# Token-first gated branches and a token-first retention tail in a three-block transformer kernel

## Chip, cores and metric

The kernel runs on one core of a Trainium2 chip. The metric is the device time of one execution in microseconds (us); a smaller time is better. TensorE (PE) multiplies matrices, VectorE (DVE) and ScalarE (ACT) do element-wise work, SyncE (SP) issues the DMAs.

## What is computed

A batch of 256 tokens of width 1024 goes through one block with three gated branches (convolution, stick-breaking attention, cross attention to a memory) and then through two hybrid layers (softmax attention with forget gates, and retention). In the reference, the parts that the change touches are these:

```python
# first block
gates = jax.nn.sigmoid(gate_pre).reshape(b, s, N_BRANCH, d)
merged = gates[:, :, 0] * y_conv + gates[:, :, 1] * y_sb + gates[:, :, 2] * y_x
x = x + merged @ w_out[l]              # y_* are [256,1024] @ [1024,1024]
# each of two hybrid layers: 4 retention heads of 128
q_r = rotary(rq); k_r = rotary(rk) * (RET_HEAD_DIM ** -0.5)
ret = retention_chunkwise(q_r, k_r, rv, gamma)
ret = (ret - mean) * rsqrt(var + GN_EPS) * ret_gn_g      # per token and head
ret_out = jax.nn.silu(rg) * ret
mixed = concatenate([fox_out, ret_out], -1)
x = layernorm(ALPHA * x + mixed @ w_out)
x = layernorm(ALPHA * x + square(relu(x @ w_ff1)) @ w_ff2)
```

## The kernel before

Every weight matrix is cut into "halves" of 1 MB (128 partitions x 2048 values). SP loads a half into one of two slots of raw, ACT rounds it to w_hi (split, L331), DVE subtracts to get w_lo (L725), both in a ring of four. Activations are kept as such pairs too (H, R, Q), and each product is three: hi x hi, lo x hi, hi x lo. Half l is split while half l - 4 is finished; SP loads half l once lo_ready has reached l - 1, that is, once the low part of half l - 2, in the same slot, is done. The order on each engine is written out by hand and every queue runs in order.

A half is multiplied in one of two forms. rows_first (products at L1282) has the weights stationary and streams 256 tokens, so the output has features in partitions: 8 x 2 x 3 = 48 matmuls with 256 columns. tokens_part and tokens_half (L1321, L1322, L1327) have 128 tokens stationary and stream 512 weight columns, so the output has tokens in partitions: 4 x 2 x 3 = 24 matmuls with 512 columns. A token-first output needs two halves (both halves of the contraction) and two PSUM banks, one for each block m of 128 tokens; results go to a ring of three banks of gps.

First block: h runs over 64 halves. Halves 36 to 59 are the gated stretch: four pairs (gate, y) for each of the branches sb, x and conv. ACT turns the gate's bank into gate with a sigmoid (L557) and copies y's to staged (L347), DVE multiplies and adds into merged (L1073 to L1077), and for the last branch ACT and DVE make Q_hi and Q_lo of it (L565, L1083). Halves 60 to 63 are w_out, token-first, then mlp_norm. The heads of the cross attention (h = 35 to 40: scores, softmax on DVE and ACT at L1010 to L1021 and L511, transposes at L1479, values at L1490) and the last norms of its queries (head_rsqrt, L351 and L353) run between the first of these halves.

A hybrid layer: l runs over 16 halves, then w_out takes four (LWO = 16 to 19), then the MLP starts at LFFN = 20. Among the halves are: rotations of queries and keys (rotate(r), L1624, DVE at L1183 to L1186, two of them after l = 11), the retention scores and masks (L1719, L1192), retention_values (L1630, L1632; b = 0 after l = 14, b = 1 after l = 15), the gate projection rg (LRG = 14 and 15, rows-first). The retention's output ro has features in partitions, so mean and variance per head are sums over partitions: matmuls with a matrix of ones (L1640, L1645), in between w_out's first two halves; ACT squares, DVE centres (L1216), and the reciprocal root is taken on whole 128x512 tiles (L742 to L746, L351, L353). ACT and DVE then write Q_hi and Q_lo (L707, L1243), for which w_out's last two halves wait. SP loads the norm's rows (load_rows) after rn_o and gn_lo. DVE does split(LWO+3) after the two centrings; split(LFFN) and split(LFFN+1) come after the last Q_lo and ahead of layer_norm (L817 to L873). layer_norm's result is transposed by TensorE (L1345).

## Time and profile before

| | |
|---|---|
| median of 3 runs | 1312.22 us (1306.88 to 1312.27) |
| profiled execution | 1308.6 us, span 1306.8 us |
| granted TensorE clock, mean | 0.990 |
| TensorE busy | 1245.1 us (95%) |
| VectorE busy | 775.6 us (59%) |
| ScalarE busy | 616.4 us (47%) |
| loads of weight halves | 196 of 1 MB, mean 166 GB/s over the span |

A line of the timeline gives the start in the span, the duration, the engine, the line of the kernel, the operation and its tiles; in brackets stands the engine's idle time before it and what ended it. The chain is the work that ended last, followed back link by link. Back-to-back instructions overlap, so durations of neighbours can add up to more than the distance of their starts; the chain's pieces do not overlap.

### The profile page before, as it was taken

The numbers are of one execution on the slowest core, as the hardware profiler recorded it, in microseconds if no ns is written. First come the engines' busy times: TensorE is split into PE (matmuls) and PEld (weight loads), VectorE is DVE, ScalarE is ACT, GpSimd is POOL, SyncE is SP. The second block draws the span as 40 slices with busy tenths as digits, with TensorE's granted clock in tenths as the row PEclk, the third lists the DMA queues.
The fourth block names the chain that finished last, engine by engine and source line by source line (L and its number), as shares of the span: only waits on it lengthen the run. The fifth ranks groups of instructions, "written<-read, shape, count | busy, mean of one in ns | idle before, by whom it ended". The sixth has DMA issues, their size and how long they took to land.

```text
span 1306.8 us, 19708 instructions
## 1 busy us (share of the span) xinstructions
PE 1245.1 (95%) x8208; PEld 1124.8 (86%) x8208; DVE 775.6 (59%) x823; ACT 616.4 (47%) x676; POOL 0.2 (0%) x4
## 2 busy tenths in 40 slices
PE   5989999999999999999999989999998998899997
PEld 5979998989999899998787868989978886789896
DVE  5566875764555565555356586555566566765545
ACT  4555554664534454444254535544435434454441
POOL 0000000000000000000000000000000000000000
PEclk9989999999999999999999999999999999999999
DMA  6644344433655356554353334655525334365550
GB/s 214 219 158 162 127 164 144 179 125 134 214 203 181 129 212 207 193 183 171 114 202 108 148 139 166 222 181 199 169 94 194 129 129 177 130 209 193 193 193 32
DMA packets 33250, 216.88 MB, mean 166 GB/s; under 512 B 4384, under 2 KB 6432, under 8 KB 7456
## 3 DMA queue, kind: packets, MB, share of 16 engines
q1 hardware_dynamic: 33184, 215.92, 47.5%
q8 instruction: 51, 0.84, 0.3%
q14 instruction: 15, 0.12, 0.0%
HBM read 214.85 MB, written 1.05 MB: 165 GB/s over the span
## 4 chain that ended last, share of the span: by engine, by line
PE 75%; DVE 11%; DMA 6%; ACT 5%; issue 2%; SPq 0%; ACTq 0%; DVEq 0%
PE gps L1282 39%; PE aps L1321 7%; PE aps L1322 7%; PE aps L1327 7%; DMA raw<-w 6%; DVE w_lo L725 4%; PE gps L1321 3%; ACT w_hi L331 3%; PE gps L1322 3%; PE gps L1327 3%; PE aps L1432 1%; DVE B L873 1%; DVE rs L863 1%; DVE B L867 1%; DVE B L817 1%
## 5 line engine op out<-in xcount | busy, mean ns | idle before, releaser
L725 DVE TENSOR_TENSOR w_lo<-raw,w_hi 128x2048 fp32r<-128x2048 f32 x200 | 449.0, 2248 | 288.1 <-ACT w_hi L331 287.8
L331 ACT ACTIVATE w_hi<-raw 128x2048 fp32r<-128x2048 f32 x200 | 374.1, 1875 | 210.9 <-DMA raw<-w 122.1
L1282 PE MATMUL gps<-H_hi,w_hi 128*128 128x256 f32 x896 | 240.9, 290 | 12.5 <-ACT H_hi L366 5.7
L1282 PE MATMUL gps<-H_hi,w_lo 128*128 128x256 f32 x896 | 236.6, 285 | 0.0
L1282 PE MATMUL gps<-R_hi,w_hi 128*128 128x256 f32 x800 | 209.2, 283 | 0.0
L1282 PE MATMUL gps<-R_hi,w_lo 128*128 128x256 f32 x800 | 209.0, 283 | 0.0
L1282 PEld LDWEIGHTS gps<-H_hi,w_hi 128*128 128x128 f32 x896 | 174.1, 194 | 16.4 <-issue 12.9
L1282 PE MATMUL gps<-H_lo,w_hi 128*128 128x256 f32 x896 | 181.4, 285 | 0.0
L1282 PEld LDWEIGHTS gps<-H_hi,w_lo 128*128 128x128 f32 x896 | 174.1, 194 | 0.7 <-issue 0.5
L1321 PE MATMUL aps<-w_hi,Q_hi 128*128 128x512 f32 x416 | 162.2, 390 | 0.8 <-DVE Q_lo L923 0.8
L1322 PE MATMUL aps<-w_lo,Q_hi 128*128 128x512 f32 x416 | 162.1, 390 | 0.0
L1282 PE MATMUL gps<-R_lo,w_hi 128*128 128x256 f32 x800 | 160.5, 283 | 0.0
L1282 PEld LDWEIGHTS gps<-R_hi,w_lo 128*128 128x128 f32 x800 | 153.5, 192 | 0.8
L1282 PEld LDWEIGHTS gps<-R_hi,w_hi 128*128 128x128 f32 x800 | 153.4, 192 | 0.8
L1282 PEld LDWEIGHTS gps<-H_lo,w_hi 128*128 128x128 f32 x896 | 141.1, 194 | 0.0
L1282 PEld LDWEIGHTS gps<-R_lo,w_hi 128*128 128x128 f32 x800 | 124.5, 192 | 0.0
L1327 PE MATMUL aps<-w_hi,Q_lo 128*128 128x512 f32 x416 | 111.2, 389 | 0.0
L1321 PEld LDWEIGHTS aps<-w_hi,Q_hi 128*128 128x128 f32 x416 | 78.2, 188 | 16.5 <-DVE Q_lo L923 1.0
L1327 PEld LDWEIGHTS aps<-w_hi,Q_lo 128*128 128x128 f32 x416 | 78.1, 188 | 16.2
L1322 PEld LDWEIGHTS aps<-w_lo,Q_hi 128*128 128x128 f32 x416 | 78.2, 188 | 15.7
L406 ACT ACTIVATE staged<-gps 128x512 f32<-128x512 f32 x42 | 25.0, 596 | 103.6 <-PE gps L1282 103.6
L347 ACT ACTIVATE B<-gps 128x512 f32<-128x512 f32 x56 | 32.3, 588 | 72.2 <-PE gps L1282 63.3
(223 smaller groups left out, 1377.2 us busy)
## 6 DMA issues: line engine op xcount, KB each, us to landing
raw<-w SPq DMA_DIRECT2D x196, 1024.0 KB, 4.9
B<-rows SPq DMA_DIRECT2D x4, 1024.0 KB, 4.5
B<-x_t SPq DMA_DIRECT2D x2, 512.0 KB, 4.6
B<-mem_t SPq DMA_DIRECT2D x1, 1024.0 KB, 9.1
B<-x SPq DMA_DIRECT2D x1, 1024.0 KB, 7.7
B<-con SPq DMA_DIRECT2D x1, 1024.0 KB, 9.6
out<-B SPq DMA_DIRECT2D x4, 256.0 KB, 2.0
B<-rows SPq DMA_DIRECT2D x1, 512.0 KB, 6.2
```

What stands on the lines that cost most here:

```text
L331: act.activation(w_hi[:, ring(l), 0:n], raw[:, raw_slot(l), 0:n], ACT.Copy)\
L347: act.activation(dst, src, ACT.Copy, scale=scale).then_inc(s["evac"], 1)
L406: act.activation(staged[:, a, :], up_bank(par_, a), ACT.Relu)\
L725: dve.tensor_tensor(w_lo[:, ring(l), 0:n], raw[:, raw_slot(l), 0:n], w_hi[:, ring(l), 0:n].bitcast(F32), ALU.subtract)\
L817: ins = dve.scalar_tensor_tensor(t, t, scale, out, ALU.mult, ALU.add)
L863: st.mark(dve.bn_stats(stats[:, m, 6 * j:6 * j + 6], chunk(X, m, j)))
L867: st.mark(dve.scalar_tensor_tensor(t, t, stats[:, m, 12:13], g_row[:, 512 * j:512 * (j + 1)], ALU.subtract, ALU.mult))
L873: dve.scalar_tensor_tensor(t, t, stats[:, m, 17:18], b_row[:, 512 * j:512 * (j + 1)], ALU.mult, ALU.add).then_inc(s["t_z"], 1)
L1282: return pe.matmul(gps[:, bank_, nt * T:(nt + 1) * T], w[:, r, c:c + P], op[:, k, :], start=start, stop=stop, skip_group_check=True)
L1321: pe.matmul(out, x, w_hi[:, r, c], start=(start and k == ks[0]), stop=False)
L1322: pe.matmul(out, x, w_lo[:, r, c], start=False, stop=False)
L1327: ins = pe.matmul(out, op_lo[:, 4 * g + k, rows], w_hi[:, r, c], start=False, stop=(stop and k == ks[-1]))
```

## The change

The weights of gates and branch outputs are laid out for token-first products, in pairs of halves: for each branch and each 512 columns two halves of the gate, then two of y. All 24 halves become tokens_half. ACT evacuates both token blocks after the second half of a pair, DVE gates them into merged, now with tokens in partitions, and TensorE transposes merged (turn_merged: 8 transposes after half 56, 8 among w_out's first half) for Q_hi and Q_lo.

In the hybrid layers rg is token-first as well and stays in PSUM. retention_values gives tokens in partitions, both blocks after l = 15. Mean and variance come from bn_stats and bn_aggr per head, the root is taken on 4 values per token, ACT normalises with scale and bias per token, and DVE multiplies with the gate, which it has multiplied with the gain from gn_row (a new broadcast load of 256 KB per layer, which SP issues once fx_l has reached 4). TensorE transposes the result for Q_hi and Q_lo (turn_retention). The matmuls for mean and variance go, and the squares and the full-size Newton steps with them. DVE does split(LWO+3) after gn_gated. w_out's last two halves go block by block. rotate(2) uses its own bank and does not wait for rt_x any more. In the diff, removed lines are left out in the longer pieces; they are those of the kernel printed above.

```diff
@@ -293,8 +294,11 @@
                     sp.wait_ge(s["gn_lo"], 2 * ly)
                 sp.dma_start(lpar[:, :], par2[ly]).then_inc(s["lpar_loaded"], 16)
 
-                for i in range(2, 10):
+                for i in range(2, 9):
                     load_pair(i)
+                sp.wait_ge(s["fx_l"], 4 * ly + 4)
+                sp.dma_start(gn_row, rows3[ly:ly + 1, :].to_broadcast([P, 4 * P])).then_inc(s["gn_row_loaded"], 16)
+                load_pair(9)
                 sp.wait_ge(s["rn_o"], 2 * ly + 2)
                 load_rows(0)
                 load_pair(10)
+                    if (h - 36) % 4 == 1:
+                        for m in range(2):
+                            act.wait_ge(s["gemm_done"], h + 1)
+                            act.wait_ge(s["staged_free"], staged_n + m - 1)
+                            act.activation(gate[:, m, :], bank(h - 1 + m), ACT.Sigmoid).then_inc(s["evac"], 1)
+                    elif (h - 36) % 4 == 3:
+                        for m in range(2):
+                            act.wait_ge(s["staged_free"], staged_n - 1)
+                            evac(staged[:, m, :], bank(h - 1 + m), h + 1)
+                            staged_n += 1
                 elif h == WO1:
                     act.preload_act_table_set("natural_log_exp_and_others")
+                if h in (GATED["conv"] + 4, WO1):
+                    for m in range(2):
+                        j = int(h == WO1)
+                        act.wait_ge(s["mg_tr"], 2 * j + m + 1)
...
                     if l == LRG + 1:
+                        for m in range(2):
+                            act.wait_ge(s["gemm_done"], done)
+                            act.activation(rsig[:, m, :], bank(LRG + m), ACT.Sigmoid).then_inc(s["rg_sig"], 1)
+                        act.preload_act_table_set("natural_log_exp_and_others")
+                        for m in range(2):
+                            gs = gn_stats[:, m, :]
+                            act.wait_ge(s["gn_v"], ly * 2 + m + 1)
+                            st.mark(act.activation(gs[:, 52:56], gs[:, 32:36], ACT.Ln))
+                            st.settle()
+                            act.activation(gs[:, 36:40], gs[:, 52:56], ACT.Exp, scale=-0.5).then_inc(s["gn_log"], 1)
+                        for m in range(2):
+                            gs = gn_stats[:, m, :]
+                            act.wait_ge(s["gn_r"], ly * 2 + m + 1)
+                            for h in range(RET_HEADS):
+                                c = slice(h * P, (h + 1) * P)
+                                ins = act.activation(ro[:, m, c], retention_out(m)[:, c], ACT.Identity,
+                                                     scale=gs[:, 44 + h:45 + h], bias=gs[:, 48 + h:49 + h])
+                            ins.then_inc(s["gn_n"], 1)
                         split(h0, LWO + 3)
+                        for m in range(2):
+                            act.wait_ge(s["gn_tr"], ly * 2 + m + 1)
+                            act.activation(operand(Q_hi, m, 1), four(retention_turned(m)), ACT.Copy)\
+                               .then_inc(s["gn_hi"], 1)
                         split(h0, LFFN)
                         split(h0, LFFN + 1)
                 layer_norm(ly * 2, R_hi)
...
+                elif 36 <= h < WO1 and (h - 36) % 4 == 3:
+                    for m in range(2):
+                        dve.wait_ge(s["evac"], h + m)
+                        t = chunk(merged, m, (h - 36) // 4 % 2)
+                        sg, gg = staged[:, m, :], gate[:, m, :]
+                        staged_n += 1
+                        if h < GATED["x"]:
+                            dve.tensor_tensor(t, sg, gg, ALU.mult).then_inc(s["staged_free"], 1)
+                        else:
+                            st.mark(dve.tensor_tensor(sg, sg, gg, ALU.mult))
+                            st.settle()
+                            dve.tensor_tensor(t, t, sg, ALU.add).then_inc(s["staged_free"], 1)
+                            if h > GATED["conv"]:
+                                dve.wait_ge(s["staged_free"], staged_n)
+                                dve.sem_inc(s["mg"], 1)
...
+                    if r >= 1:
+                        dve.wait_ge(s["rt_x"], ly * 4 + r)
                     st.mark(dve.tensor_tensor(rott, two(rotated(r)), sin_b, ALU.mult))
...
+                def gn_moments(m):
+                    gs, o = gn_stats[:, m, :], retention_out(m)
+                    dve.wait_ge(s["rn_o"], ly * 2 + m + 1)
+                    for h in range(RET_HEADS):
+                        ins = dve.bn_stats(gs[:, 6 * h:6 * h + 6], o[:, h * P:(h + 1) * P])
+                    st.mark(ins)
+                    st.settle()
+                    for h in range(RET_HEADS):
+                        ins = dve.bn_aggr(gs[:, 24 + 2 * h:26 + 2 * h], gs[:, 6 * h:6 * h + 6])
+                    st.mark(ins)
+                    st.settle()
+                    dve.tensor_scalar(gs[:, 32:36], gs[:, 25:32:2], EPS_GN, None, ALU.add).then_inc(s["gn_v"], 1)
+                    dve.wait_ge(s["gn_v"], ly * 2 + m + 1)
+
+                def gn_root(m):
+                    gs = gn_stats[:, m, :]
+                    dve.wait_ge(s["gn_log"], ly * 2 + m + 1)
+                    newton(gs[:, 32:36], gs[:, 36:40], gs[:, 40:44], gs[:, 44:48], None)
+                    dve.scalar_tensor_tensor(gs[:, 48:52], gs[:, 24:31:2], -1.0, gs[:, 44:48], ALU.mult, ALU.mult)\
+                       .then_inc(s["gn_r"], 1)
+
+                def gated(m):
+                    dve.wait_ge(s["rg_sig"], ly * 2 + m + 1)
+                    dve.tensor_tensor(rg[:, m, :], gps[:, (LRG + m) % 3, :], rsig[:, m, :], ALU.mult)\
+                       .then_inc(s["rg_t"], 1)
+                    dve.wait_ge(s["rg_t"], ly * 2 + m + 1)
+                    st.mark(dve.tensor_tensor(rg[:, m, :], rg[:, m, :], gn_row, ALU.mult))
+
+                def gn_gated(m):
+                    dve.wait_ge(s["gn_n"], ly * 2 + m + 1)
+                    dve.tensor_tensor(ro[:, m, :], ro[:, m, :], rg[:, m, :], ALU.mult).then_inc(s["gn_y"], 1)
+
+                def gn_lo(m):
+                    dve.wait_ge(s["gn_hi"], ly * 2 + m + 1)
+                    dve.tensor_tensor(operand(Q_lo, m, 1), four(retention_turned(m)),
+                                      operand(Q_hi, m, 1).bitcast(F32), ALU.subtract).then_inc(s["gn_lo"], 1)
+
+                gn_moments(0)
+                gn_moments(1)
+                gn_root(0)
+                gn_root(1)
+                dve.wait_ge(s["gn_row_loaded"], 16 * (ly + 1))
+                gated(0)
+                gated(1)
+                st.settle()
+                gn_gated(0)
+                gn_gated(1)
+                split(h0, LWO + 3)
+                gn_lo(0)
+                gn_lo(1)
...
                 elif h < WO1:
+                    g, first = (h - 36) % 2, GATED["conv"] + 2
+                    banks = ((h - g) % 3, (h - g + 1) % 3)
+                    second_free = h - 1 if g == 0 else None
+                    if (h - 36) % 4 < 2:
+                        tokens_half(0, h, g, banks, H_hi, H_lo, second_free)
+                    elif h < GATED["conv"]:
+                        if h == GATED["sb"] + 2:
                             pe.wait_ge(s["sb_olo"], SB_PAIRS)
+                        if h == GATED["x"] + 2:
+                            pe.wait_ge(s["ox_lo"], 2)
+                        if h == GATED["x"] + 3:
+                            pe.wait_ge(s["ox_lo"], 4)
+                        tokens_half(0, h, g, banks, Q_hi, Q_lo, second_free)
                     else:
+                        if h == first:
                             pe.wait_ge(s["cv_lo"], 4)
+                        tokens_half(0, h, g, banks, R_hi, R_lo, second_free)
+                    if h == GATED["conv"] + 4:
+                        turn_merged(0, 0)
+                        turn_merged(0, 1)
                 elif h < WO1 + 2:
                     pe.wait_ge(s["lo_ready"], h + 1)
                     for m in range(2):
+                        c = m + 1 if h == WO1 else m + 3
                         ins = tokens_part(h, acc(m, h - WO1), m, 0, Q_hi, Q_lo, start=True,
+                                          hi_ready=(s["mg_lo"], c))
+                        if m == 1:
+                            ins.then_inc(s["gemm_done"], 1)
+                        if h == WO1:
+                            turn_merged(1, m)
                 elif h == WO1 + 2:
                     for m in range(2):
                         for a in range(2):
                             pe.wait_ge(s["lo_ready"], h + a + 1)
                             ins = tokens_part(h + a, acc(m, a), m, 1, Q_hi, Q_lo, stop=True,
...
-                    if r >= 1:
-                        pe.wait_ge(s["rt_x"], ly * 4 + r)
+                    if r in (1, 3):
+                        pe.wait_ge(s["rt_x"], ly * 4 + (r + 1) // 2)
...
+                def retention_values(m):
+                    o = retention_out(m)
+                    for h in range(RET_HEADS):
+                        c = slice(h * P, (h + 1) * P)
+                        ins = pe.matmul(o[:, c], inner[:, h, m * P:(m + 1) * P], rv[:, 0, c], start=(h == 0),
+                                        stop=(m == 0), skip_group_check=True)
+                        if m == 1:
+                            ins = pe.matmul(o[:, c], inner[:, h, 256:384], rv[:, 1, c], start=False, stop=True,
+                                            skip_group_check=True)
                     ins.then_inc(s["rn_o"], 1)
 
+                def turn_retention(m):
+                    pe.wait_ge(s["gn_y"], ly * 2 + m + 1)
+                    for h in range(RET_HEADS):
+                        c = slice(h * P, (h + 1) * P)
+                        ins = pe.transpose(retention_turned(m)[:, c], ro[:, m, c], ident)
+                    ins.then_inc(s["gn_tr"], 1)
...
                     tokens_part(LWO, wo_acc(1, 0), 1, 0, Q_hi, Q_lo, start=True)\
                         .then_inc(s["gemm_done"], 1)
                     half_ready(LWO + 1)
+                    pe.wait_ge(s["rg_t"], ly * 2 + 1)
                     tokens_part(LWO + 1, wo_acc(0, 1), 0, 0, Q_hi, Q_lo, start=True)
+                    turn_retention(0)
+                    pe.wait_ge(s["rg_t"], ly * 2 + 2)
                     tokens_part(LWO + 1, wo_acc(1, 1), 1, 0, Q_hi, Q_lo, start=True)\
                         .then_inc(s["gemm_done"], 1)
+                    turn_retention(1)
+                    for m in range(2):
                         for a in range(2):
                             half_ready(LWO + 2 + a)
+                            ins = tokens_part(LWO + 2 + a, wo_acc(m, a), m, 1, Q_hi, Q_lo, stop=True,
+                                              hi_ready=(s["gn_hi"], ly * 2 + m + 1),
+                                              lo_ready=(s["gn_lo"], ly * 2 + m + 1))
+                            ins.then_inc(s["acc_ready" if m == 0 else "gemm_done"], 1)
 
                 pe.wait_ge(s["ffn_relu"], ly * 16 + 16)
...
                         rotate(3)
+                        pe.wait_ge(s["rt_x"], ly * 4 + 3)
                         retention_scores(0)
                         pe.wait_ge(s["fx_oe"], ly * 4 + 3)
                         retention_scores(1)
-                    if l == 14:
+                    if l == 15:
                         pe.wait_ge(s["evac"], e0 + evac_count(LRV + 1))
+                        pe.wait_ge(s["rn_m"], ly * 4 + 4)
                         retention_values(0)
-                    if l == 15:
                         retention_values(1)
-                        retention_mean(0)
                 w_out()
                 ffn(h0, LFFN, ly + 1, X, s["t_z"], 4 * (1 + 2 * ly))
 
```

## Rows read from the trace of the kernel before

**Rows 1.** The page: busy time of TensorE; shares of the chain that ended last.

```profile
PE 1245.1 (95%) x8208; PEld 1124.8 (86%) x8208; DVE 775.6 (59%) x823; ACT 616.4 (47%) x676; POOL 0.2 (0%) x4
...
PE 75%; DVE 11%; DMA 6%; ACT 5%; issue 2%; SPq 0%; ACTq 0%; DVEq 0%
```

**Rows 2.** Waits of TensorE: who waited for whom, us in total, times, longest.

```profile
PE aps L1345 <- DVE B L873: 7.3, 5, 2.8
...
PE gps L1321 <- ACT Q_hi L707: 5.7, 4, 1.6
PE aps L1624 <- DVE B L1186: 5.6, 2, 2.8
...
PE aps L1479 <- DVE B L1021: 2.8, 2, 1.5
```

**Rows 3.** The chain in order of time, 330 to 470: start, us, what.

```profile
329.96 94.80 PE gps L1282 x790
...
426.60 0.91 PE aps L1327 x4
...
429.32 0.91 PE aps L1327 x4
```

**Rows 4.** Busy time in the gated stretch: stretch, length, engines, clock, DMA.

```profile
315.00:425.00 110.00, 110.00 (x916) 109.93 (x915) 58.93 (x42) 49.28 (x46) 0.00 (x0) 1.00 0.54 188
```

**Rows 5.** DMA issues: count, KB each, median us from issue to landing.

```profile
raw<-w SPq DMA_DIRECT2D x196, 1024.0 KB, 4.9
```

**Rows 6.** Timeline of DVE and ACT, last gated half: start, us, instruction.

```profile
426.22 0.69 DVE L1077 TENSOR_TENSOR B<-B,staged 128x512 f32<-128x512 f32 x1
...
427.00 0.63 ACT L565 ACTIVATE Q_hi<-B 128x512 fp32r<-128x512 f32 x1 [1.54 <-DVEq L1081]
```

**Rows 7.** Timeline of TensorE and ACT beside the cross attention, 275 to 290.

```profile
287.92 0.66 PE L1479 MATMUL aps<-cst,B 128*128 128x128 f32 x4 [1.53 <-DVE B L1021]
...
275.63 1.28 ACT L557 ACT_TABLE_LOAD   x1
```

**Rows 8.** The chain in order of time, 738 to 787.

```profile
738.02 0.22 PE aps L1632 x2
...
738.90 5.75 PE gps L1282 x48
...
753.32 0.86 PE aps L1645 x2
...
786.76 0.45 PE aps L1345 x4
```

**Rows 9.** Timeline of TensorE, first layer, where the MLP begins.

```profile
777.64 0.66 PE L1345 MATMUL aps<-cst,B 128*128 128x128 f32 x4 [2.78 <-DVE B L873]
...
781.28 0.63 PE L1322 MATMUL gps<-w_lo,R_hi 128*128 128x512 f32 x1
```

**Rows 10.** Timeline of DVE, first layer, 731 to 777.

```profile
731.48 0.28 DVE L1193 TENSOR_TENSOR B<-aps,B 128x128 f32<-128x128 f32 x1
...
751.21 2.28 DVE L725 TENSOR_TENSOR w_lo<-raw,w_hi 128x2048 fp32r<-128x2048 f32 x1
...
772.52 0.68 DVE L817 SCALAR_TENSOR_TENSOR B<-B,gps 128x512 f32<-128x512 f32 x1
...
775.28 0.21 DVE L878 BATCH_NORM_AGGREGATE rs<-rs 128x2 f32<-128x12 f32 x1
...
776.25 0.16 DVE L742 SCALAR_TENSOR_TENSOR rs<-rs 128x1 f32<-128x1 f32 x1
```

**Rows 11.** Timeline of ACT, first layer, 703 to 766.

```profile
703.88 0.40 ACT L643 ACTIVATE spb<-spb,small 128x128 f32<-128x128 f32 x1 [3.59 <-DVE small L1161]
...
748.42 1.28 ACT L695 ACT_TABLE_LOAD   x1
749.72 1.06 ACT L695 ACTIVATE sqh<-B 128x1024 f32<-128x1024 f32 x1
...
766.18 3.70 ACT L331 ACTIVATE w_hi<-raw 128x2048 fp32r<-128x2048 f32 x2
```

214 lines of the change are left out of this document (43 added, 171 removed).

## The prediction

> **What bounds the kernel now.** I began with the page: TensorE is busy for 95% of the span and holds three quarters of the chain that ended last [rows 1]. So a part of the change is worth what it takes off TensorE's row of matmuls, or off the few places where that row stands still. The second view was therefore TensorE's waits in total [rows 2]: about 60 us of the span are no matmul, and most of that is the start of the program. Of the rest four pairs bear on this change: 7.3 us before the transposes that open an MLP (L1345), 5.7 us before w_out's retention half (L1321), 5.6 us before the third rotation (L1624), 2.8 us before the cross attention's transposes (L1479). The third view was the chain itself. Where nothing interrupts, a 256-column matmul takes 94.80/790 = 0.120 us and a 512-column one (429.32 - 426.60)/12 = 0.227 us [rows 3]. A weight half is 48 of the first or 24 of the second, so 5.76 us rows-first and 5.44 us token-first. That both forms occur in this trace, at full clock, is the base of the prediction.
>
> **Part 1, the gated branches: 24 halves token-first.** 24 x 0.32 = 7.7 us off a stretch in which TensorE is busy for 110.00 of 110 us [rows 4]. Supply must keep up: a slot of raw is filled in 4.9 us [rows 5], ACT rounds for 1.9, DVE subtracts for 2.3, some 9.3 us with the hand-overs, and two slots serve two halves in 10.9 us. It holds, with 1.6 us in hand. The three-bank ring must keep up too: the second bank of a pair is used by the next pair 2.72 us after the last half ended. Now a half's copy, gate product and sum are all done at 426.91, 2.15 us after the half's end at 329.96 + 94.80 = 424.76 [rows 3, 6]; the copy alone is out before its 1.45 us of DVE work begin, at 0.7. The first copy of a pair comes out just as early in the new order, since ACT's split ahead of it ended long before; a first gate adds a table load of 1.28 us [rows 7] and is out by 2.2 us. So no wait, with 0.5 us in hand where it is tightest.
>
> At its beginning this stretch overlaps the cross attention. There ACT loads tables three times around one head, 1.28 us each: for the sigmoid (the row stands for the three), for Ln, for Exp [rows 7]. With the gate's second half coming later, no sigmoid stands ahead of head_rsqrt(7), and the two loads on its way (2.56 us) go; the chain Ln, Exp, Newton, maximum, exponential, scaling that ends in the 1.53 us wait of the second transpose [rows 7] comes forward by more than this wait. I take 1.5 us. The first transpose's wait, 2.8 - 1.5 = 1.3 us [rows 2, 7], hangs on ACT and DVE alone and eats the 0.3 us of half 36.
>
> Added: 16 transposes of merged, four in 0.45 us [rows 8], so 1.8 us. The last of them: the merged chunk of token block 0 is ready at about 2.3 us after the last y half (ACT sees it at 427.00, 2.24 us after the half) [rows 6], and TensorE first does 2.72 us of w_out, so no wait. But ACT has split(63) (1.9), the table load (1.28) and then the copies; the low part of block 0 comes at 6.8 us where TensorE stands ready at 6.35: 0.45 us lost. Sum of part 1: 7.7 - 0.3 + 1.5 - 1.8 - 0.45 = 6.7 us. The four halves of w_out and what follows keep their order, and their last sums are covered as before.
>
> **Part 2, rotations and values, per layer.** rotate(2) goes to another bank than rotate(1) and no longer waits for rt_x: 2.8 us off TensorE [rows 2]. What is late next is DVE, which does rotations 1 and 2 in a row; the scores of the last fox pair need its third rt_x only a whole half later, so the gain stays. Two rg halves token-first: 0.64 us. retention_values(0), 1.3 us of TensorE's time, moves from before half 15 behind it. Call the end of half 15 A; A comes 2.8 + 0.6 + 1.3 = 4.7 us earlier. Before, A is 738.90 + 5.75 = 744.65 and TensorE starts the MLP's transposes at 777.64: A + 33.0 [rows 8, 9].
>
> **Part 3, from A to the MLP, per layer.** Two engines race, and I follow both. TensorE: the values are now 12 products of 128 columns at 0.22 [rows 8], 2.6 us; the w_out halves are 8 x 2.72 = 21.8; 8 transposes 0.9. The four 512-column sums of mean and variance (0.86 each [rows 8], 3.4 us) are gone. It ends at A + 25.3 if never held.
> DVE: rn_o of block 0 at A + 0.9. bn_stats and bn_aggr on 128 columns do not occur before; the nearest rows are a 128x128 product at 0.28 and an aggregation at 0.21 [rows 10]. With these, a block is 4 x 0.28 + 4 x 0.21 + 0.2 = 2.2 us; from below, with 0.16 for each small one, 1.4; from above, if bn_stats cost what a 512-column instruction does (0.69), 3.8. I take 2.2, since the width is that of the first row. Both blocks: A + 5.3. Two roots on 4 columns, 8 small instructions of 0.16 plus hand-over [rows 10]: A + 6.9. In the meantime ACT has done load, two sigmoids, load (1.28 + 1.1 + 1.28 from A, so A + 3.8) and Ln/Exp; its 8 normalising copies of 128x128 at 0.40 at most [rows 11] end 0.3 us before DVE asks. gated x2 are four instructions of 0.69, gn_gated two [rows 6]: A + 11.0. Then comes split(LWO+3), 2.3 us [rows 10]: A + 13.3, and behind this one instruction three parties wait: gn_lo, TensorE's last two halves and, through lo_ready, the load of LFFN+1. gn_y of block 0 is at A + 10.3 against TensorE at A + 10.8; gn_lo(0) at A + 14.0 against its use at A + 16.5. TensorE is never held.
> The start of the layer norm is set by the load: 13.3 + 4.9 (landing [rows 5]) + 1.9 (ACT, half of 3.70 [rows 11]) + 2.3 = A + 22.4. Before, DVE's layer norm needs 777.64 - 772.52 = 5.1 us to the first transposes [rows 9, 10]: A + 27.5. Before, A + 33.0; so 5.5 us per layer. What went is the tail of 512-column Newton steps on DVE and both of w_out's waits; what ends last now is SP's queue through DVE. The loads of gn_row (SP waits for fx_l ahead of the pair 18, 19) and of the norm rows stay off the path: all three are issued before anyone misses them.
> A word on the tables: two switches fall in this part, and in the trace ACT's next instruction starts 0.02 us behind the 1.28 us load [rows 11]. The Trainium skill, "ScalarE: Activation LUTs", What ACT_TABLE_LOAD costs, gives 1283 ns plus a drain of about 1380 ns for every switch; by it Ln would come 2.8 us later here, near A + 6.6, the roots about 1.5 us later, and each layer would gain some 1.5 us less. The row decides, and no drain is in it.
>
> **Sum.** 6.7 + 2 x (4.7 + 5.5) = 27.1 us. The profiled execution took 1308.6 us (span 1306.8), so 1281.5. It lies between the fastest (1306.88) and the median (1312.22) of the three timed; against the median the same sum would give 1285, which the range takes in.
>
> **Rivals.**
> A, the clock comes back. Ahead of the MLP TensorE stands for 2.78 us and then runs six matmuls of 0.63 us [rows 9] like the one shown, at the 1.2 GHz level, where they last 0.39 at 2.4 GHz: 0.2 us more from start to start, together 1.2 us a layer. With a stand of 2.2 us and w_out's two others gone the drop may not come, and DVE's back-to-back instructions may cost 0.1 less each: 2 x (1.2 + 1) = 4.4 us more, 1277. For it: the shorter pauses at 762 and 766 did no such thing. Against it: the pause that remains is nearly as long.
> B, DVE's chain is longer (bn_stats at 0.69, waits between the small ones): 1.6 us a block from above, 3 us a layer, 1287.5. Every microsecond of it reaches the load of LFFN+1.
> C, the bank ring stalls in the gated stretch: if each pair waited 0.5 us or more for the first copy, half of the 7.7 would go, and with the cross attention's gain all of part 1: 1288.
> The Trainium skill, "TensorE: Matmul & The Clock Gate", Back-to-back issue gap, has N/2.4 + 2.5 ns for an isolated matmul: 109 and 216 ns, so 5.24 against 5.18 us a half and 1.7 us for all 28 halves. A pace at which the forms are equal is rival C's time too, by another cause; the trace gives 0.120 and 0.227 in hundreds of matmuls, so I leave it 2 in 100.
> D, slower. The one path that could do it is DVE's order in the retention tail: split(LWO+3) is now behind the whole group norm instead of ahead of most of it, and the load of LFFN+1 behind it. It decides from 13.3 + 27.1/2, that is, a low part ready only at A + 26.9: the norm's instructions at over twice their length. At A + 30, with part 1 worth nothing, it is 2 x (16.7 - 10.2) = 13 us slower, 1322. Nothing in the rows is near that.
> E, the change removes matmuls' time but supply takes it back everywhere (loads at 6.5 us instead of 4.9): within 0.5% of before, about 1308.
>
> **Chances.** Forecast 0.60 (1278 to 1286), A 0.14, B 0.14, C with the equal pace 0.08, E 0.02, D 0.02. Range: down to A with a quicker run, 1273; up to B and C with the median's offset of 3.6 us, 1292. About 0.5% (6.6 us) is what a measurement of this kernel can tell from no change; faster 0.95, same 0.03, slower 0.02.
>
> **What would show it.** In the new trace: 128x512 groups in the gated stretch with 2.72 us per twelve and no ACT release of the second bank (else C); no table load between half 36 and the second head's exponential; no wait of rotate(2) for DVE; bn_stats at 0.28 (else B); no PE wait for gn_hi; raw<-w of LFFN+1 as the last link before the layer norm. Wrong would be: TensorE held at turn_retention, or DVE's w_lo as releaser in the gated stretch.

## The result, and the profile after

| | before | after |
|---|---|---|
| median | 1310.83 us (1306.88 to 1312.27, 4 runs) | 1272.78 us (1271.03 to 1274.98, 4 runs) |
| profiled execution, span | 1308.6, 1306.8 us | 1271.03, 1269.2 us |
| mean granted clock over the runs | 0.990 in the profiled one | 0.993 to 0.997 |
| TensorE busy | 1245.1 us (95%) | 1225.7 us (97%) |

The ratio of after to before is 0.9716 [0.9692, 0.974]: 38 us faster. Runs of before made beside the later kernels had medians of 1308.88 (15 runs), 1308.35 (13 runs) and 1311.02 (7 runs), so the gain is 36 to 38 us, where the sum had 27.1. The median lies 8.7 us below the predicted 1281.5, 4.2 below rival A's 1277 and 0.2 below the range's lower end. Profiled against profiled it is 37.6 us of the span.

The page of after, busy times and shares of the chain that ended last (before: [rows 1]):

```profile
PE 1225.7 (97%) x7568; PEld 1085.8 (86%) x7568; DVE 769.7 (61%) x853; ACT 608.6 (48%) x679; POOL 0.2 (0%) x4
...
PE 73%; DVE 12%; DMA 7%; ACT 5%; issue 2%; SPq 0%; ACTq 0%; DVEq 0%
```

TensorE's waits in after: who waited for whom, us in total, times, longest (before: [rows 2]):

```profile
PE aps L1354 <- DVE B L878: 6.1, 7, 1.6
...
PE aps L1330 <- DVE Q_lo L928: 1.8, 2, 1.1
...
PE aps L1496 <- DVE B L1026: 0.9, 1, 0.9
```

The wait for the rotation and those for Q_hi in w_out are gone from the list. The one ahead of the transposes (L1354) has lost 1.2 us in all, and the one for Q_lo inside an MLP's opening (L928) has come up in both layers; before it was 0.8 us, once.

The gain can be cut into stretches by pieces of TensorE's chain that stand at the same places of both programs: the first unbroken piece of block 1, the start of each loop over FFN halves (96 matmuls), and in each layer the half behind the first rotation (48 matmuls), its mark. The stretch up to layer 2's mark is counted from a later piece of the same loop, the one 112.10 us behind its start in both kernels. For layer 1 of after the last two are these lines of the chain (start, us, what), 112.35 us apart:

```profile
681.36 5.75 PE gps L1291 x48
...
793.71 11.51 PE gps L1291 x96
```

Distances in us, from the profiled execution of each kernel (the kernels after the first two are the experiments below). The last column is the time lost to the lower clock, as explained behind the table:

| kernel | start to first piece | from it to block 1's FFN | FFN to layer 1's mark | mark to FFN | FFN + 112.10 to layer 2's mark | mark to FFN | lost to the clock |
|---|---|---|---|---|---|---|---|
| before | 104.31 | 379.41 | 209.57 | 123.69 | 99.22 | 124.47 | 10.2 |
| after | 100.70 | 372.84 | 207.82 | 112.35 | 95.99 | 113.36 | 1.7 |
| branches_alone | 102.27 | 372.74 | 208.42 | 123.45 | 97.69 | 126.70 | 10.2 |
| rotate_alone | 102.59 | 380.11 | 209.22 | 121.93 | 96.79 | 121.54 | 10.2 |
| layers_alone | 101.11 | 380.01 | 209.80 | 112.42 | 97.51 | 112.98 | 3.4 |
| load_alone | 101.00 | 380.55 | 209.79 | 128.03 | 97.58 | 126.00 | 10.3 |
| moments_twice | 101.99 | 372.54 | 208.12 | 114.64 | 95.84 | 114.86 | 6.8 |
| split20_early | 100.16 | 372.36 | 208.11 | 112.53 | 96.00 | 112.95 | 3.4 |
| tail_reordered | 102.58 | 372.81 | 208.24 | 110.90 | 95.84 | 111.36 | 3.4 |
| pause_filled | 102.65 | 380.28 | 209.62 | 127.04 | 96.06 | 129.44 | 11.9 |
| rotate_waits | 100.35 | 373.20 | 207.85 | 116.81 | 95.97 | 116.26 | 6.9 |

From before to after: 3.6 + 6.6 + 1.8 + 11.3 + 3.2 + 11.1 = 37.6 us, the whole difference. The three stretches that were edited give 29.0, against 27.1 in the sum. The other 8.6 lie where nothing was edited.

Part of it comes from TensorE's clock. Windows of before and then of after, the same work 82 to 90 us from the start (stretch, length, busy time of PE, PEld, DVE, ACT and POOL, granted clock, DMA share, GB/s):

```profile
80.00:90.00 10.00, 6.53 (x20) 4.75 (x20) 4.59 (x2) 4.79 (x4) 0.00 (x0) 0.66 0.57 201
```

```profile
80.00:90.00 10.00, 8.14 (x40) 6.11 (x39) 5.36 (x3) 7.86 (x8) 0.00 (x0) 1.00 0.61 206
```

In before TensorE had stood for 3.5 us there and then ran at the lower level (1.2 GHz) for a while; in after it stood for 1.9 us and kept 2.4 GHz. From the first matmul behind this pause to the first piece before has 20.84 us and after 18.12, so the clock makes 2.7 of the 3.6 us of this stretch. In windows of 2 us through the whole of each profiled execution, I added (1 - granted clock) x length over those below full clock, without the last 10 us of a kernel, in which TensorE has little left to do: the last column of the table. Nearly every drop is 1.7 us or twice that. By stretches, before has 3.4 at the start, 1.7 ahead of layer 1, 1.7 in each layer and 1.7 ahead of layer 2; after has the last alone.

This sum is an upper bound of what the clock costs, since part of a drop falls on work that something else paces, and the traces show both cases. Ahead of layer 2's mark the drop of before stands on TensorE's part of the chain and costs 1.5 us; the one of after stands at 958 us, where the chain is in a load. Before and then after (start, us, what):

```profile
994.24 6.33 DMA raw<-w
...
1011.05 7.24 PE gps L1282 x48
```

```profile
970.76 4.80 DMA raw<-w
...
986.04 5.75 PE gps L1291 x48
```

The other 1.5 us of the 3.2 in this stretch are the load: behind the late one of before TensorE waits 2.0 us for a head's probabilities (spb, L1602), and its drop stands behind this pause; in after the wait is 0.3 us. Other executions have 95.8 to 97.7 us in this stretch, with and without the edits, so both are chance. Ahead of layer 1's mark the chain of before is inside a load while the clock is low (648 to 654 us), so the drop costs nothing there, and the 1.75 us of this stretch are the loads on the chain, this one above all:

```profile
647.89 6.04 DMA raw<-w
```

```profile
637.67 4.73 DMA raw<-w
```

In the MLP's opening a single drop costs nothing either by the time the FFN loop starts. In layer 1 before has one at 778 us and needs 39.3 us from the first transposes to the loop; after has none and needs 39.4 (754.29 to 793.71):

```profile
754.29 0.66 PE L1354 MATMUL aps<-cst,B 128*128 128x128 f32 x4 [1.07 <-DVE B L878]
```

The others agree: with one such drop 39.1 to 39.4 us in layer 1 and 39.7 to 40.2 in layer 2 (branches_alone, moments_twice, rotate_waits; before, rotate_alone, load_alone, moments_twice), without one 39.4 to 39.7 and 39.9 to 40.3 (after, layers_alone, split20_early; in layer 2 rotate_waits too). With 3.4 us lost it is 40.6 to 42.2, and in pause_filled 41.0 without a drop and 42.2 with one, behind waits for Q_lo of 2.3 and 1.8 us. These waits suggest that loads, and the low parts made of them, pace this stretch: after waits 0.63 and 1.12 us for Q_lo in it. By this the gain of the three edited stretches is the work's, 6.6 + 11.3 + 11.1 = 29.0 us, and the clock and the loads of this pair of executions make the other 8.6.

Over more executions the layers gain rather more. Before, branches_alone and load_alone, which have the layers of before, show 123.5 to 128.0 us from a mark to the FFN loop, 125.4 on average, with one to three drops' worth (1.7 to 5.1 us) in each; after, layers_alone and split20_early show 112.4 to 113.4, 112.8 on average, and no drop. That is 12.6 us a layer instead of 11.2, and the likely place of the clock's gain in the layers: the second and third drop, not the one that the profile of before has.

### The profile page after: what moved, and what is told of

It reads as the page before. It is cut to its first block, busy times and chain, and to the rows that moved or that the text cites. A ratio compares the mean times of both kernels' runs of the same rounds, so it can differ in the third digit from the quotient of the medians.

```text
span 1269.2 us, 18459 instructions
## 1 busy us (share of the span) xinstructions
PE 1225.7 (97%) x7568; PEld 1085.8 (86%) x7568; DVE 769.7 (61%) x853; ACT 608.6 (48%) x679; POOL 0.2 (0%) x4
## 4 chain that ended last, share of the span: by engine, by line
PE 73%; DVE 12%; DMA 7%; ACT 5%; issue 2%; SPq 0%; ACTq 0%; DVEq 0%
PE gps L1291 27%; DMA raw<-w 7%; PE aps L1330 7%; PE aps L1331 7%; PE aps L1336 7%; PE gps L1330 6%; PE gps L1331 6%; PE gps L1336 6%; DVE w_lo L730 5%; ACT w_hi L335 3%; DVE B L878 1%; PE aps L1449 1%; DVE rs L868 1%; DVE B L872 1%; DVE B L822 1%
## 5 line engine op out<-in xcount | busy, mean ns | idle before, releaser
L1291 PE MATMUL gps<-R_hi,w_hi 128*128 128x256 f32 x736 | 192.5, 283 | 0.0
L1291 PE MATMUL gps<-R_hi,w_lo 128*128 128x256 f32 x736 | 192.3, 283 | 0.0
L1291 PE MATMUL gps<-H_hi,w_hi 128*128 128x256 f32 x640 | 172.7, 291 | 11.5 <-ACT H_hi L370 5.9
L1291 PE MATMUL gps<-H_hi,w_lo 128*128 128x256 f32 x640 | 169.3, 286 | 0.0
L1291 PEld LDWEIGHTS gps<-H_hi,w_hi 128*128 128x128 f32 x640 | 124.5, 195 | 15.1 <-issue 13.2
L1291 PE MATMUL gps<-H_lo,w_hi 128*128 128x256 f32 x640 | 129.5, 285 | 0.0
L1291 PEld LDWEIGHTS gps<-H_hi,w_lo 128*128 128x128 f32 x640 | 124.7, 195 | 0.6 <-issue 0.5
L1291 PEld LDWEIGHTS gps<-H_lo,w_hi 128*128 128x128 f32 x640 | 100.9, 195 | 0.0
L1330 PE MATMUL gps<-w_hi,H_hi 128*128 128x512 f32 x224 | 90.1, 402 | 2.9 <-ACT B L351 1.9
L1331 PE MATMUL gps<-w_lo,H_hi 128*128 128x512 f32 x224 | 87.4, 390 | 0.0
```

The source lines that it names most:

```text
L1291: return pe.matmul(gps[:, bank_, nt * T:(nt + 1) * T], w[:, r, c:c + P], op[:, k, :], start=start, stop=stop, skip_group_check=True)
L1330: pe.matmul(out, x, w_hi[:, r, c], start=(start and k == ks[0]), stop=False)
L1331: pe.matmul(out, x, w_lo[:, r, c], start=False, stop=False)
```

## The experiments

**Each part alone.** branches_alone is before with the gated branches and w_out of block 1 from after; layers_alone is before with all that the change does in the hybrid layers. The edit of each is its share of the diff above. 

> The kernel before, with the token-first gated branches alone; the hybrid layers stay as they were. My steps give 6.7 us (24 halves at 5.44 instead of 5.76 us, 1.5 us of wait in the cross attention, less 16 transposes and the waits around them): about 1304. Between the last gated half's end and the start of the MLP the trace of the changed kernel shows two waits, 0.3 us and 0.5 us, and both should be here. Rival (something that the change does to the stretches it doesn't touch is worth the 9 us that my sum did not have): 1295 to 1299, with the start of the program or the landing of loads earlier than in the kernel before.

> The changed kernel with its gated branches put back to rows-first; so the kernel before plus the rotation, the token-first gate projection, values and group norm. My steps give 2 x 10.2 = 20.4 us; the trace of the changed kernel shows 11.2 us from the middle of one layer to the middle of its MLP: 22.4 us, so 1288 to 1290. If branches_alone and this one together give less than the 38 us of the whole, the rest is either chance of those runs or hangs on both together; if each has a surplus of its own, at stretches without any edit, it is in the layout or in the phase of the clock. Rival (the retention tail is worth 30 us or more by itself): under 1283.

branches_alone took 1299.22 us (1298.14 to 1301.14, 5 runs), ratio 0.9923 [0.9899, 0.9948]; layers_alone 1282.11 (1280.44 to 1285.36, 4 runs), ratio 0.98 [0.9768, 0.9831]. Against 1308.88 that is 9.7 and 26.8 us, together 36.5: the parts add up to the whole, 36 to 38. Both came out faster than my steps had them (1304, and 1288 to 1290), where the rivals had 1295 to 1299 and under 1283. In the table the branches' stretch has 372.4 to 373.2 in the kernels with them and 379.4 to 380.6 in those without, so 6.2 to 8.2 us, 7.3 by the medians. The surplus of branches_alone is not the clock: its runs have 0.988 to 0.991, no more than those of before, and 10.2 us lost like before. 0.8 to 2.0 us of it may be the stretch ahead of layer 1's mark: the six kernels with the token-first branches have 207.8 to 208.4 us there and the five without 209.2 to 209.8, and the load that takes 6.04 us in before takes 5.96 to 6.42 in rotate_alone, load_alone and pause_filled and 4.73 to 4.92 in all six. Why it lands sooner no run shows. layers_alone has 22.8 us of its gain in the two layers, by this profile, and 3.4 us lost to the clock instead of 10.2, with a mean clock of 0.991 to 0.996 over its runs: what the change gains from the clock comes with this part.

**The rotation's wait alone.** In rotate_alone DVE takes over the order and TensorE only waits where the bank is the same:

```diff
@@ rotate(r) on DVE
                     dve.wait_ge(s["rt_mm"], ly * 4 + (r + 1))
+                    if r >= 1:
+                        dve.wait_ge(s["rt_x"], ly * 4 + r)
@@ rotate(r) on TensorE
-                    if r >= 1:
-                        pe.wait_ge(s["rt_x"], ly * 4 + r)
+                    if r in (1, 3):
+                        pe.wait_ge(s["rt_x"], ly * 4 + (r + 1) // 2)
@@ after rotate(3)
+                        pe.wait_ge(s["rt_x"], ly * 4 + 3)
```

> The kernel before, with one thing of the change: rotate(2) on TensorE does not wait for rt_x any more (the scores after it do). My steps: the 2.8 us wait of L1624 goes in each of two layers and the first matmul behind it loses its slow start, 5.6 to 6.4 us in all; TensorE's end moves by as much, since DVE's rotations are needed only a half later: 1304.5 to 1305.5 against 1310.8. Rival (the time is given back, because the fox and retention chains on DVE end the layer): a shorter wait at L1624 and longer ones at L1602 or in front of the group norm, gain under 2 us.

Measured: 1300.17 us (1299.45 to 1301.18, 5 runs), ratio 0.9934 [0.9913, 0.9954]. From the mark of the layer to half 14 the chain has 33.19 and 33.18 us instead of 36.25 and 36.24: 3.06 us a layer, none of it given back up to there. That is 6.1 of the 8.7 us by which the medians differ (1304.5 to 1305.5 was expected); the other 2.6 have no place in the work of these stretches, nor in the clock, which is 0.989 to 0.992 over the runs and loses 10.2 us like before.

**The wait put back into after.** rotate_waits tells the pause from the clock:

```diff
-                    if r in (1, 3):
-                        pe.wait_ge(s["rt_x"], ly * 4 + (r + 1) // 2)
+                    if r >= 1:
+                        pe.wait_ge(s["rt_x"], ly * 4 + r)
```

> The kernel after, with one wait put back: TensorE waits for rt_x, the second rotation's last DVE instruction, ahead of the third rotation (the bank stays the new one). Nothing is left out. It puts one pause of 2.8 to 3.1 us per layer back and nothing else. Theory 1, the clock follows the pauses: 6.1 us for the pauses and some 1.7 us of lower clock behind each, so 1271.9 + 9.5 = about 1281, and the mean granted clock falls to 0.991 or 0.992. Theory 2, only the pauses count: about 1278, the clock as after (0.993 to 0.997), and no bin below full clock behind the third rotation. Theory 3, the rotation was hidden anyway once the rest of the layer is shorter: 1272 to 1274. The distance from the layer's first value piece (the fox part) to half 14 should go from 33.2 back to 36.2 us in theories 1 and 2.

Measured: 1278.16 us (1276.93 to 1280.97, 4 runs), ratio 0.9759 [0.973, 0.9787], mean clock 0.991 to 0.995. The median is 5.4 us above after's and so at theory 2's 1278, while the clocks lie between the two theories' and the two layers differ. TensorE's timeline at the third rotation in layer 1 and in layer 2 (start, us, instruction, idle time before it):

```profile
699.97 2.08 PE L1653 MATMUL aps<-B 128*128 128x512 f32 x2 [2.81 <-DVE B L1195]
...
1024.85 1.12 PE L1653 MATMUL aps<-B 128*128 128x512 f32 x2 [2.80 <-DVE B L1195]
```

And windows around the two places (columns as above, the granted clock third from the end):

```profile
698.00:702.00 4.00, 2.03 (x3) 1.00 (x4) 1.88 (x3) 0.94 (x1) 0.00 (x0) 0.68 0.68 250
...
1022.00:1028.00 6.00, 3.20 (x13) 2.30 (x13) 4.71 (x8) 1.83 (x2) 0.00 (x0) 1.00 0.52 175
```

The same pause, 2.8 us, is followed by the lower clock in one layer (two matmuls take 2.08 us) and not in the other (1.12). Up to the FFN loop of layer 1 this kernel is 4.5 us behind after (798.21 against 793.71), and from there to that of layer 2 only 2.9 (324.33 against 321.45). Layer 1 has a second drop at 760 us, ahead of the MLP, which after has not. So theory 1 holds in layer 1 and theory 2 in layer 2: the price of a pause is its length, and some 1.5 us on top where a drop follows at the rotation (4.5 less the 2.9 to 3.1 of the pause). The drop at 760 us adds nothing, since this kernel needs 39.4 us from the transposes to the FFN loop, as after does without it.

**A pause filled.** In before, three matmuls without use (512 columns into a bank that is free; the result is unchanged) run ahead of the MLP's transposes, where TensorE had stood for 2.78 us:

```diff
+                    for _ in range(3):
+                        pe.matmul(aps[:, 3, :], ones, ro[:, 2:4, :], start=True, stop=True)
```

> The kernel before with three extra products of ones with ro behind w_out in each hybrid layer, into a bank that nobody reads: 2.6 us of TensorE's work in the 2.8 us in which it waits for the layer norm. In every execution of a kernel with the old tail that I have a trace of, the clock was granted at 0.5 for 3 to 7 us behind this pause, at a cost of 1.7 us or a multiple of it; behind the new tail never. If the pause is the cause: no granted clock under 1.0 in the MLP's opening, and 3.4 us or somewhat more gained, 1303 to 1306 against 1308.9. If the pause is not the cause (or the extra products delay the transposes): no gain, or 0.2 to 1 us lost.

Measured: 1306.26 us (1301.6 to 1313.02, 10 runs), ratio 0.998 [0.9967, 0.9993]. The drop that followed the old pause is gone, but in the profiled execution others stand at places that had none in before (pause_filled, windows):

```profile
710.00:714.00 4.00, 2.88 (x5) 1.65 (x6) 1.80 (x4) 0.10 (x1) 0.00 (x0) 0.64 0.75 262
780.00:784.00 4.00, 3.98 (x20) 3.36 (x21) 3.90 (x7) 0.60 (x1) 0.00 (x0) 1.00 0.00 0
```

Its ten runs are of use for another question, what the clock is worth, since their clocks lie far apart with the same program: 0.989 gave 1313.02 us, 0.991 gave 1305.95, 0.994 gave 1306.58 and 1305.58, 0.996 gave 1301.6; a straight line through the ten has 1.15 us less for each 0.001 more. The slope is a correlation, not a price; the 35 runs of before that were made beside the other kernels give 0.8 us in the same way. So this pause was one contributor among several, about 2 us in all. The profiled execution was the slowest of the ten, so its row of the table is not to be read for the layers.

**The group norm's statistics twice.** moments_twice is after, with each block's bn_stats and bn_aggr done twice; the result is unchanged.

```diff
+                    for _ in range(2):
+                        for h in range(RET_HEADS):
+                            ins = dve.bn_stats(gs[:, 6 * h:6 * h + 6], o[:, h * P:(h + 1) * P])
...
+                            ins = dve.bn_aggr(gs[:, 24 + 2 * h:26 + 2 * h], gs[:, 6 * h:6 * h + 6])
```

> The changed kernel with bn_stats, bn_aggr and their hand-overs done twice per block; the result is the same. In the changed kernel a block of moments took 1.5 us, so 2.7 us more of DVE work per layer. Theory 1, my prediction's (DVE's chain through split(LWO+3) and the load of LFFN+1 starts the layer norm): all of it arrives, 5 us in all, 1278 against 1272.8, and w_lo of LFFN+1 moves by 2.7 us. Theory 2 (TensorE's row of w_out with its transposes, and ACT's order behind the last of them, start it; DVE had 1.7 us in hand at the first transpose): TensorE is held for about 1 us at the first transpose and the layer norm moves by that, 2 to 3 us in all, 1275.

Measured: 1277.39 us (1275.94 to 1278.73, 4 runs), ratio 0.9771 [0.9752, 0.979], 4.6 us above after; mean clock 0.991 to 0.992. Each layer gets 2.7 us more of statistics, and the layer norm starts 23.6 us after half 15 where after has 21.4: 2.2 of the 2.7 arrive. In layer 2, where the load of LFFN+1 is missed by 0.8 us in after, 1.5 arrive by the table. TensorE's timeline at the MLP's opening, layer 1:

```profile
757.85 0.66 PE L1355 MATMUL aps<-cst,B 128*128 128x128 f32 x4 [2.31 <-DVE B L878]
759.30 1.03 PE L1355 MATMUL aps<-cst,B 128*128 128x128 f32 x4 [0.80 <-DVE B L878]
```

The pause is back at 2.3 us, and the second group of transposes runs at the lower level (1.03 against 0.66); both layers have a drop here again, which costs nothing up to the FFN loop (39.4 and 39.7 us). So the length of DVE's chain is what sets this end, and most of it reaches the time: 4.6 of 5.4 us by the medians, as theory 1 had it (1278).

**What the layer norm waits for.** Two re-orderings of after. split20_early puts split(LFFN) between the two blocks' copies of the turned retention, on ACT and on DVE. tail_reordered does this and also puts split(LWO+3) back ahead of the last multiplications:

```diff
@@ DVE
+                split(h0, LWO + 3)
                 gn_gated(0)
                 gn_gated(1)
-                split(h0, LWO + 3)
                 gn_lo(0)
-                gn_lo(1)
                 split(h0, LFFN)
+                gn_lo(1)
```

> The changed kernel with the split of LFFN ahead of the second block's Q_hi on ACT and of its Q_lo on DVE. Theory 1 (the load of LFFN+1 sets the layer norm): that load lands at the same time, ACT rounds it 0.2 us earlier at most, nothing is gained: 1272 to 1273. Theory 2 (ACT's and DVE's order sets it, the two splits one behind the other): DVE does the first of its two splits while it waits, the second ends with the load, landing + 1.9 + 2.3 us; gain at most 0.2 us a layer, since both meet within 0.2 us. A gain of 1 us or more a layer would refute both.

> split20_early, and split(LWO+3) besides ahead of the normalising copies on ACT and ahead of gn_gated on DVE. The load of LFFN+1 is issued 1.3 us earlier; TensorE finds its first transpose's input 0.3 to 0.8 us late. If the load sets the layer norm: its start comes 1.0 to 1.3 us earlier in each layer, less what TensorE's sums come late, 1 to 2 us in all, 1271. If TensorE's row sets it: 0.5 us a layer slower, 1274.

Measured: split20_early 1271.47 us (1270.08 to 1272.37, 4 runs), ratio 0.9724 [0.9706, 0.9743]; tail_reordered 1269.03 (1267.67 to 1269.76, 4 runs), ratio 0.97 [0.9681, 0.972]. (On ACT split(LWO+3) stands ahead of the normalising copies then.) ACT's timeline of split20_early, layer 1:

```profile
741.61 0.60 ACT L712 ACTIVATE Q_hi<-aps 128x512 fp32r<-128x512 f32 x1 [0.79 <-PE aps L1671]
744.22 1.92 ACT L335 ACTIVATE w_hi<-raw 128x2048 fp32r<-128x2048 f32 x1 [2.01 <-DMA raw<-w]
```

With the engines' own work out of the way, the load of LFFN+1 alone is waited for, 2.0 us of it, and the layer norm starts 21.3 us after half 15, as before the edit. Only when split(LWO+3), on which that load depends, comes earlier does the start move. DVE of tail_reordered:

```profile
738.40 2.29 DVE L731 TENSOR_TENSOR w_lo<-raw,w_hi 128x2048 fp32r<-128x2048 f32 x1
...
747.68 2.29 DVE L731 TENSOR_TENSOR w_lo<-raw,w_hi 128x2048 fp32r<-128x2048 f32 x1 [0.30 <-ACT w_hi L335]
749.89 0.68 DVE L823 SCALAR_TENSOR_TENSOR B<-B,gps 128x512 f32<-128x512 f32 x1
```

Half 15 ends at 730.1 there, so the layer norm starts 19.8 us later, 1.6 earlier than in after, for a wait of 0.41 us at turn_retention. This is the fastest kernel of the study. It shared its chip with split20_early, whose four times lie all above its own; against after, which was timed apart, the median is 3.7 us lower and the layers are 1.5 and 2.0 us shorter.

**The row of the gain alone.** load_alone is before with one more broadcast load per layer behind a wait of SP for fx_l (64 KB, a quarter of the real row).

```diff
-                for i in range(2, 10):
+                for i in range(2, 9):
                     load_pair(i)
+                sp.wait_ge(s["fx_l"], 4 * ly + 4)
+                sp.dma_start(gn_row[:, :], rows3[ly:ly + 1, 0:P].to_broadcast([P, P])).then_inc(s["gn_row_loaded"], 16)
+                load_pair(9)
```

> The kernel before with one more input array and one more small broadcast load per layer, issued by SP where the changed kernel issues the load of the gain (after fx_l, 64 KB instead of 256 KB, into a place nobody reads); the computation is that of before. My theory: no effect, within 0.3% of before (1307 to 1314), and its profile shows how much the start of the program, the clock and the landing times differ between two executions without any edit there. Rival (the place of arrays in memory or the extra load makes the surplus of 9 us): 1300 to 1304.

Measured: 1309.74 us (1305.36 to 1313.55, 10 runs), ratio 1.0008 [0.9989, 1.0027]: nothing, as the prediction had it for this queue. The layers of its profiled execution are longer (128.03 and 126.00), with 5.1 and 3.4 us lost to the clock in them. This profile alone would have blamed the load; the ten runs don't.

## Why the prediction came out as it did

**The gated branches, 6.7 us.** Right. The chain has 2.72 us per twelve matmuls (274.65 to 277.39) without a break; by the table 6.2 to 8.2 us. Rival C's stall does not occur. The cross attention's transposes wait 0.9 us in all, where 2.8 stood before and 1.3 were forecast. The chain of after around w_out's second block of matmuls shows the small loss that the sum had at 0.45, at the place it named:

```profile
412.58 0.61 ACT staged L351
...
416.34 2.29 DVE w_lo L730
418.64 0.61 DVE Q_lo L1090
...
421.47 0.92 PE aps L1336 x4
```

DVE's split(63) stands between the sums and Q_lo, and TensorE waits 0.5 us for it. The cause differs in part: I had ACT's table load as the last link, and it is DVE's subtraction.

**Rotation and values, 4.7 us a layer.** Right: half 15 ends at 727.81, which is 16.84 us earlier than before, of which 11.93 were gained ahead of the layer's mark, so 4.9. Of the rotation's 2.8, 3.06 arrived.

**From half 15 to the MLP, 5.5 us a layer.** This is the term of the sum that was mis-sized: 6.5 measured, at full clock (A + 26.5). DVE in after (start, us, instruction):

```profile
728.74 0.89 DVE L1225 BATCH_NORM_STATS2 rs<-aps 128x6 f32<-128x128 f32 x4 [2.02 <-PE aps L1659]
729.66 0.38 DVE L1229 BATCH_NORM_AGGREGATE rs<-rs 128x2 f32<-128x6 f32 x4
730.08 0.17 DVE L1232 TENSOR_SCALAR rs<-rs 128x4 f32<-128x4 f32 x1
...
737.67 2.29 DVE L730 TENSOR_TENSOR w_lo<-raw,w_hi 128x2048 fp32r<-128x2048 f32 x1
...
744.76 4.49 DVE L730 TENSOR_TENSOR w_lo<-raw,w_hi 128x2048 fp32r<-128x2048 f32 x2 [1.11 <-ACT w_hi L335]
749.17 0.68 DVE L822 SCALAR_TENSOR_TENSOR B<-B,gps 128x512 f32<-128x512 f32 x1
```

The row is nearly the forecast's. bn_stats does last 0.28 us by itself, but four in a row take 0.89 and four aggregations 0.38, because neighbours overlap: a block costs 1.5 us and not 2.2. I had added durations where distances of starts count, and that is most of the 1.0 us by which the term was too low; the split ends at A + 12.2 instead of 13.3, the layer norm starts at A + 21.4 instead of 22.4. Rival B, with longer statistics, is refuted by the same rows. The last link before the layer norm is named less surely than I had it: in ACT's timeline of after the load is missed by only 0.19 us in layer 1 (0.82 in layer 2),

```profile
742.32 0.60 ACT L712 ACTIVATE Q_hi<-aps 128x512 fp32r<-128x512 f32 x1 [2.59 <-PE aps L1670]
742.82 1.91 ACT L335 ACTIVATE w_hi<-raw 128x2048 fp32r<-128x2048 f32 x1
744.91 1.92 ACT L335 ACTIVATE w_hi<-raw 128x2048 fp32r<-128x2048 f32 x1 [0.19 <-DMA raw<-w]
```

behind the chain of turn_retention, Q_hi and split(LFFN), which ends 0.2 us before. The two are tied, and split20_early shows that the load, taken alone, gives the same start. Behind the transposes nothing of this is lost. Layer 1 is 4.9 + 6.5 = 11.4 us ahead at the transposes and 11.3 at the FFN loop, layer 2 10.8 and 11.1, where the sum had 10.2. How the opening is paced by supply I had not followed: TensorE waits 0.80 us at the next block's transposes (763.37) and 0.63 us for Q_lo (782.50), where before does neither, and in the chain of after stands a load that takes 5.96 us to land, with DVE and ACT in line ahead of it and behind it:

```profile
766.50 4.50 DVE w_lo L730 x2
771.02 5.96 DMA raw<-w
...
781.16 1.29 DVE Q_lo L928 x2
```

**The tables.** ACT of after at the first root:

```profile
724.40 1.28 ACT L693 ACT_TABLE_LOAD   x1
727.84 1.08 ACT L693 ACTIVATE sqh<-gps 128x512 f32<-128x512 f32 x2 [2.16 <-PE gps L1336]
728.95 1.28 ACT L694 ACT_TABLE_LOAD   x1
```

The first load was done while ACT waited for TensorE, so that the sigmoids began at once and both tables and sigmoids were done at A + 2.4, where I had A + 3.8. By the Trainium skill, "ScalarE: Activation LUTs", What ACT_TABLE_LOAD costs, each switch has some 1380 ns of drain besides the load. Ln starts at 730.28, 0.05 us behind the end of the second load, and this load starts 0.03 us behind the end of the sigmoids, so the trace disagrees with the page here as it did before.

**The clock, rival A.** This term I had set at nothing in the sum, and here about half of the distance between 27.1 and 36 to 38 us lies. I asked of the clock only at the MLP's opening, saw 1.2 us a layer there, and gave the rival 0.14. Its condition came true: the pause is 1.07 and 1.61 us in after and no drop follows. Yet it was priced wrongly. On TensorE's row that drop costs 1.5 us (from the first transposes to the seventh matmul 4.85 us in before, 3.34 in after), and none of it arrives at the FFN loop (39.3 and 39.4 us). That the time came near the rival's 1277 is luck, for the surplus lies elsewhere: at the start, ahead of the layers' marks, and in further drops in the layers, which the one profile that I had did not show.

How large the clock's part is over the runs is known only roughly. The mean clock went from 0.9898 (35 runs of before, 0.986 to 0.993) to 0.9953 (four of after, 0.993 to 0.997). At 0.8 to 1.15 us for each 0.001 this is 4.4 to 6.3 us. With the 29.0 us of work it makes 33 to 35 of the 36 to 38 us; loads that land sooner, as in the stretch ahead of layer 1's mark, are of the kind of thing that fills the rest, and this remainder is not settled. The higher mean clock is lasting, since the two ranges only touch. It comes with the layers' part: the three kernels with the new tail and no pause put back that are not after itself (layers_alone, split20_early, tail_reordered) lose 3.4 us, the five with the old tail 10.2 to 11.9, and the two with a pause put back 6.8 and 6.9. The drop at the start is chance: its stretch lasts 100.2 to 101.1 us without one, 102.0 to 102.7 with one, and 104.3 with the two of before, whatever was edited. What exactly decides whether a pause is followed by a drop stays open: rotate_waits has the same pause with and without one, and filling one pause moved the drops.

**D and E** have no sign for them: DVE's split(LWO+3) was ready 14.7 us before D's point, and supply takes back nothing of the work up to the FFN loops; in the MLP's openings it makes the drop's absence worth nothing.

## What to carry to other kernels

Compare the two forms of a product by the spacing of matmuls in long unbroken stretches, and cost a chain of small instructions by the distance of their starts, not by their durations. When a change removes pauses of TensorE of 2 to 3 us, add up the granted clock's loss over the whole program of before, and of more than one execution: here the clock was worth some 15 to 20% of the work's gain on top, estimated from the mean clocks, and it does not show at the place of the edit alone. Then ask of each drop whether the chain is on TensorE there: ahead of layer 2 a drop cost 1.5 us, in the MLP's openings, which loads pace, nothing. Where an engine's split gates a load that the next stage needs, move the split first and the load's wait follows; that was worth 2.4 us against split20_early on the same chip, and 3.7 against after's own times.

## What the runs showed of the hardware

Nearly every drop of the clock lost 1.7 us of full-speed time or twice that, wherever it stood in the eleven kernels; 1.5 us of it arrived where TensorE's row was the chain (48 matmuls in 7.24 us instead of 5.75) and nothing where loads paced (39.3 us with it, 39.4 without). A pause of 2.8 us was followed by one in one layer and not in the next, in the same execution. bn_stats on 128 columns lasts 0.28 us and repeats every 0.2; bn_aggr of one such result lasts 0.15 us and repeats every 0.08, and the larger one before lasts 0.21.
